# Statistics, decay chains, combining weights and the low-rank product of a fused encoder layer

## What is computed

```python
z = rms_norm(x, norm_mix_g) @ w_in           # all projections in one
gq, gk, gv, gg, gaf, gab, aq, ak, av, gate_a, gate_b = split(z)
# per direction; gaf, gab have 16 columns
la_f = log_sigmoid(gaf @ gla_wa2_f + gla_ba_f) / 16
la_b = log_sigmoid(gab @ gla_wa2_b + gla_ba_b) / 16
b  = cumsum(chunks(log_a))                   # gla_direction
qe, ke = q * exp(b), k * exp(-b)             # then chunked gated attention
o_a = rms_norm(o_f + o_b) * silu(gg)
# dilated attention, groups (window, dilation) = (128,1), (512,4), (2048,16)
o_g = softmax(q_g k_g^T / sqrt(128) - slope * dist) @ v_g     # with lse_g per query
wts = softmax(stack(lse_g), axis=0)          # over the three groups
o_att = sum(wts[g] * o_g)
merged = sigmoid(gate_a) * (o_a @ w_branch_a) + sigmoid(gate_b) * (o_att @ w_branch_b)
x += merged @ w_out;  x += relu(rms_norm(x) @ w1)^2 @ w2
x += sigmoid(rms_norm(x) @ w_pg) * (p @ w_pp)
```

## Time and profile before

| | us |
|---|---|
| three runs, median (lowest to highest) | 2895.54 (2891.09 to 2896.45) |
| the profiled execution | 2890.55 |
| its span, first to last instruction | 2889.0 |
| PE busy in the span | 2758.6 |
| DVE busy, ACT busy | 1172.1, 975.6 |

### The profile page before, as it was taken

How to read it: one execution, slowest core, us unless ns; L and a number is a source line. 1 busy time by engine, 2 the same in 40 slices (tenths; PEclk the granted TensorE clock), 3 DMA queues, 4 the chain that set the end, 5 groups by cost and what they waited for, 6 DMA issues and landing times.

```text
span 2889.0 us, 40495 instructions
## 1 busy us (share of the span) xinstructions
PE 2758.6 (95%) x14806; PEld 2365.4 (82%) x14806; DVE 1172.1 (41%) x1953; ACT 975.6 (34%) x1635; POOL 157.1 (5%) x248
## 2 busy tenths in 40 slices
PE   5999899998999899998999999999999999999798
PEld 5887788877888688886888888788888888888687
DVE  3234432344333433335433341645444544444533
ACT  4454135542454324443343332421121122122422
POOL 2000000010000100010010000000000000000000
PEclk9999999999999899999999999999999999999899
DMA  3122221231212212122162321111111111111021
GB/s 97 30 31 31 59 76 30 31 56 43 67 30 31 60 34 72 30 30 61 41 233 91 113 73 56 55 36 36 40 40 36 36 36 44 36 36 36 17 73 56
DMA packets 176575, 153.19 MB, mean 53 GB/s; under 512 B 13744, under 2 KB 155392, under 8 KB 176448
## 3 DMA queue, kind: packets, MB, share of 16 engines
q1 hardware_dynamic: 153824, 94.38, 12.0%
q0 software_dynamic: 16352, 57.00, 7.4%
q10 hardware_dynamic: 6272, 0.15, 0.1%
HBM read 127.48 MB, written 23.78 MB: 52 GB/s over the span
## 4 chain that ended last, share of the span: by engine, by line
PE 84%; DVE 6%; ACT 4%; issue 3%; DMA 2%; ACTq 0%; POOL 0%; DVEq 0%; SPq 0%; POOLq 0%
PE bank L695 24%; PE bank L697 24%; PE bank L696 24%; PE bank L802 2%; PE bank L783 1%; PE bank L884 1%; PE bank L871 1%; DMA work<-weight_scratch 1%; DVE work L1499 1%; PE bank L793 1%; PE bank L931 1%; DVE work L1479 1%; PE bank L845 1%; PE bank L880 1%; PE bank L770 1%
## 5 line engine op out<-in xcount | busy, mean ns | idle before, releaser
L695 PE MATMUL bank<-act_hi,w_hi 128*128 128x512 f32 (+1 forms) x3192 | 1189.4, 373 | 27.4 <-ACT work L1208 15.9
L697 PE MATMUL bank<-act_hi,w_lo 128*128 128x512 f32 (+1 forms) x3192 | 1140.9, 357 | 0.0
L696 PE MATMUL bank<-act_lo,w_hi 128*128 128x512 f32 (+1 forms) x3192 | 1140.9, 357 | 0.0
L695 PEld LDWEIGHTS bank<-act_hi,w_hi 128*128 128x128 f32 x3192 | 609.7, 191 | 112.5 <-ACT work L1208 17.3
L697 PEld LDWEIGHTS bank<-act_hi,w_lo 128*128 128x128 f32 x3192 | 608.2, 191 | 88.8
L696 PEld LDWEIGHTS bank<-act_lo,w_hi 128*128 128x128 f32 x3192 | 610.4, 191 | 75.7
L1016 ACT ACTIVATE w_hi<-w_raw 128x1024 fp32r<-128x1024 f32 (+2 forms) x179 | 180.1, 1006 | 435.3 <-PE bank L697 393.0
L1352 DVE TENSOR_TENSOR w_lo<-w_raw,w_hi 128x1024 fp32r<-128x1024 f32 (+2 forms) x181 | 210.9, 1165 | 232.2 <-ACT w_hi L1016 226.6
L695 PE MATMUL bank<-u_hi,w_hi 128*128 128x512 f32 (+1 forms) x816 | 289.6, 355 | 2.4 <-DVE work L1708 2.4
L696 PE MATMUL bank<-u_lo,w_hi 128*128 128x512 f32 (+1 forms) x816 | 289.5, 355 | 0.0
L697 PE MATMUL bank<-u_hi,w_lo 128*128 128x512 f32 (+1 forms) x816 | 289.0, 354 | 0.0
(11 more groups left out here) (224 smaller groups left out, 2399.9 us busy)
## 6 DMA issues: line engine op xcount, KB each, us to landing
w_raw<-in_w_in_dram SPq DMA_DIRECT2D x76, 512.0 KB, 3.9
w_raw<-in_w_mlp_dram SPq DMA_DIRECT2D x64, 512.0 KB, 3.8
gate_scratch<-work POOLq DMA_DIRECT2D x16, 640.0 KB, 3.2
work<-gate_scratch POOLq DMA_DIRECT2D x16, 640.0 KB, 6.5
work<-weight_scratch POOLq DMA_DIRECT2D x12, 640.0 KB, 6.5
oa_scratch<-work POOLq DMA_DIRECT2D x8, 640.0 KB, 5.1
work<-oa_scratch POOLq DMA_DIRECT2D x8, 640.0 KB, 8.3
x_in<-in_x_sample_dram SPq DMA_DIRECT2D x8, 512.0 KB, 8.0
```

Of the source, the lines that this page charges most:

```text
L695: nc.tensor.matmul(out, wh, rh, start=first and k == 0, stop=False, skip_group_check=True)
L696: nc.tensor.matmul(out, wh, rl, start=False, stop=False, skip_group_check=True)
L697: mm = nc.tensor.matmul(out, wl, rh, start=False, stop=k == kt - 1, skip_group_check=True)
```

## The change

Six things are done.

- The third group's statistics stay on the chip. Its transpose, copy and six stores are gone; the other two groups are stored to `stat_scratch` as [token, 4] and loaded back in the third group's query order by four DMAs; DVE uses `st` as it is. So the weights' rows also lie in query order, and the weighting reads them through a view that brings them to token order (`tokens`, `query_order`), in two instructions a group where there was one.
- `T_CW` goes from 292 to 264, and POOL stores and loads the weights before it refills the carry row. The rows for groups 0 and 1 lie in z rows 1 and 2, so ACT's evacuation of slab 13 waits for the combination (`ob_ready`).
- The combination stands at tick 303, between the two scans.
- The decay chains have a pair of rows each, and their steps interleave: both y, both Exp, then both Ln at tick 286, the scans at 292 and 317.
- The low-rank product is one fp32r matmul a chunk of 96 rows: high, low and high part of `lowrank` against low, high and high part of `wa2`. The parts of `wa2` are made once a head, at tick 100, by four ACT and two DVE instructions of 32 rows, those of `lowrank` once, ahead of the heads.
- v's transposes go to ticks 322 to 337, and the products with the chunk's end, both of them, to tick 341.

```diff
-        T_LR = (268, 287)
-        T_DECAY = (277, 334)
-        T_QK = (281, 339)
-        T_CW = 292
-        T_COMBINE = 318
-        T_VT = (332, 335, 338, 341, 344)
+        T_LR, T_Y, T_ABS, T_EXP, T_LN = (268, 275), (272, 280), (274, 282), (277, 285), 286
+        T_SCAN, T_DECAY, T_QK, T_KEND = (292, 317), (303, 328), (328, 335), 341
+        T_CW, T_COMBINE = 264, 303
+        T_VT, T_VN = (322, 325, 330, 334, 337), (327, 328, 334, 340, 341)
...
+        def query_order(row):
+
+            return (row.rearrange("p (j l n) -> p l n j", j=2, n=NT)[:, :, 0:8, :],
+                    row.rearrange("p (j l n) -> p l n j", j=8, n=NT)[:, :, 8:NT, :])
...
-        WB = (6, 7, 9)
+        wb_row = (work[:, 1, :], work[:, 2, :], ar[:, 9, :])
+        Y_ROW, B_ROW = (10, 2), (11, 7)
...
+                for j in range(2):
+                    pool.dma_start(cst[64 * j:64 * j + 64, 0:8, :], sample[j]).then_inc(cst_loaded, 16)
+                for b in range(2):
+                    pool.dma_start(cst[:, 8 + b, :], prompt[b]).then_inc(cst_loaded, 16)
...
                     for c, (t0, tw) in enumerate(CHUNKS):
-                        mm = nc.tensor.matmul(bank[(3, 4, 7)[c]][:, 0:tw], wa2[32 * d:32 * d + RANK, :],
-                                              lowrank[32 * d:32 * d + RANK, t0:t0 + tw], start=True, stop=True)
+                        mm = nc.tensor.matmul(bank[(3, 4, 7)[c]][:, 0:tw], wa2[:, d, :],
+                                              lowrank[:, t0:t0 + tw], start=True, stop=True)
...
+                if tick == T_LN:
+                    for d in range(2):
+                        A(ar[:, B_ROW[d], :], ar[:, B_ROW[d], :], ACT.Ln, bias=ones[:, 0:1]).then_inc(prep_a, 1)
...
+                        if tt == 13 and c == 0:
+                            act.wait_ge(ob_ready, h + 2)
...
                 if tick == T_CW:
-                    dve.wait_ge(cst_loaded, 16 * h + 16)
+                    dve.wait_ge(cst_loaded, 64 * h + 64)
+                    dve.wait_ge(exp_done, 30 * h + 31)
...
+                if tick == T_COMBINE:
+                    dve.wait_ge(wb_loaded, 48 * h + 48)
+                    for g in range(3):
+                        for o, w in zip(tokens(ar[:, 3 + g, :]), query_order(wb_row[g])):
+                            v_.tensor_tensor(o, o, w, ALU.mult).then_inc(dve_own, 1)
+                            dve.wait_ge(dve_own, own.value())
...
+                if tick in T_VN:
+                    i = T_VN.index(tick)
                     dve.wait_ge(gvt_done, 5 * h + i + 2)
...
+                if tick == T_KEND:
+                    dve.wait_ge(prep_a, 6 * h + 7)
+                    for d in range(2):
```

More of the change, by code:

```diff
@@ L26 @@
 P = 128
[L28 removed]
+MAP_BYTES = 212832
 EPS = 1e-6
@@ L575, in _ @@
                 nc.gpsimd.memset(carry[:, :, 0:1], 0.0).then_inc(carry_ready, 1)
[L576 removed]
+                for g in range(2):
                     store_stats(h, g)
[L579 removed]
+                pool.wait_ge(stat_stored, 16 * 8 * (h + 1) + 16)
                 pool.sem_inc(pool_passed, 1)
[L581 to L588, removed]
+                sample = stat_d[0:TS, :].rearrange("(l b j) m -> j l b m", b=8, j=2)
+                prompt = stat_d[TS:T, :].rearrange("(l b j) m -> b j l m", b=2, j=8)
+                for j in range(2):
+                    pool.dma_start(cst[64 * j:64 * j + 64, 0:8, :], sample[j]).then_inc(cst_loaded, 16)
+                for b in range(2):
+                    pool.dma_start(cst[:, 8 + b, :], prompt[b]).then_inc(cst_loaded, 16)
                 pool.wait_ge(cw_ready, h + 2)
@@ L1066, in _ @@
                 act.wait_ge(mm_done, c + 2)
-                A(lowrank[:, t0:t0 + tw], bank[c][0:48, 0:tw], ACT.Copy).then_inc(evac, 1)
+                for r0 in (0, 64):
+                    A(lowrank[r0:r0 + 32, t0:t0 + tw], bank[c][0:32, 0:tw], ACT.Copy).then_inc(lr_high, 1)
+            act.wait_ge(evac, 4)
             act.wait_ge(const_pool, 2)
@@ L1110, in gla_steps @@
             def gla_steps(h, tick):
+                if tick == T_WA2:
+                    act.wait_ge(head_loaded, 64 * (h + 1))
+                    act.wait_ge(lr_done, 2 * h + 1)
+                    for d, raw in enumerate((wa2_raw[32:64, :], wa2_raw[64:96, :])):
+                        A(wa2[32:64, d, :], raw, ACT.Copy)
+                        A(wa2[64:96, d, :], raw, ACT.Copy).then_inc(wa2_high, 1)
                 if tick == T_CW + 1:
@@ L1388, in _ @@
             x_lows(2)
+            for c, (t0, tw) in enumerate(CHUNKS):
+                dve.wait_ge(lr_high, 2 * c + 2)
+                v_.tensor_tensor(lowrank[32:64, t0:t0 + tw], bank[c][0:32, 0:tw], lowrank[0:32, t0:t0 + tw].bitcast(F32),
+                                 ALU.subtract).then_inc(evac, 1)
             dve.wait_ge(const_pool, 2)
@@ L1475, in gla_steps @@
                                      ALU.mult).then_inc(cw_ready, 1)
-                if tick == T_COMBINE:
-                    dve.wait_ge(wb_loaded, 48 * h + 48)
-                    for g in range(3):
-                        v_.tensor_tensor(ar[:, 3 + g, :], ar[:, 3 + g, :], ar[:, WB[g], :], ALU.mult).then_inc(dve_own, 1)
-                        dve.wait_ge(dve_own, own.value())
-                    v_.tensor_tensor(ar[:, 3, :], ar[:, 3, :], ar[:, 4, :], ALU.add).then_inc(dve_own, 1)
-                    dve.wait_ge(dve_own, own.value())
-                    v_.tensor_tensor(ar[:, WB[2], :], ar[:, 3, :], ar[:, 5, :], ALU.add).then_inc(ob_ready, 1)
```

163 lines of the change are left out of this document (89 added, 74 removed).

## The result

The changed kernel takes **2821.4 us** (median of 4 runs, 2820.9 to 2823.4), the kernel before in the same session 2896.0 (2891.1 to 2897.6): ratio 0.9744, 95% interval 0.9731 to 0.9758, 74.6 us less. The two profiled executions are 2890.55 and 2821.26 us, 69.3 apart. The forecast was 2836, its range 2812 to 2858.

A forecast was written before the change was run, and what follows sets the result against it. DVE's chain to v's first copy was taken to bound ticks 264 to 352: PE's floor 56.1, waits 0.2 and 7, half clock 2.8. From 81.0 to 66.2 us a head, times four 59 us, gives 2836 us, range 2812 to 2858.

The forecast's parts named there:

- Where: Ticks 264 to 352 of each head: 81.0 us become 66.2, 14.8 us a head; elsewhere nothing PE waits for changes.
- PE's floor: PE's own work at full clock in ticks 264 to 352: 59.7 us before, 56.1 after.
- The statistics and the transfer: Statistics loaded ahead of tick 264; the weights' 12.6 us store and load hidden, there 13 us before use: cost nothing.
- slower rival: DVE waits at tick 264 for late statistics loads, a loss from 15 us late on; 2920 us at worst, 6%.
- Scan 0: Its tick's work starts 23.8 us after tick 264, behind both Ln, an evacuation and `w_lo`; done at 29.9.
- The combination: DVE's weighting and additions after scan 0: 11.0 us with strided reads, bounds 8.1 and 13.7, ready at 40.9.
- The stall: PE at the third transposes (tick 330) waits for v's first copy from 42.0 to 49.0: 7 us, before about 10.8.
- The half clock: PE's slower clock after the stall at the third transposes: 2.8 us a head.
- ACT: Evacuation wait of 0.2 us at tick 320, before some 2.8 a head; ACT idle 5 us before slab 13, costing nothing.
- offset of 5 us: Added to the 2831.5 us forecast for the profiled execution, since the three runs' median before was 5 higher: 2836.
- the view costs little: Strided weighting nearly free: combination 8.1 us, stall 4, window 61.6 to 63.4, 2818 to 2825 us; 13%.
- DVE isn't the bound: v's first copy ready at 42, 7 us sooner; window 56.1, gain 24.9 a head, 2796 us; 5%.

The follow-up runs named there:

- serial_chains: Changed kernel with the two directions' decay chains one after the other, scan 0 at tick 282, four table loads a head: 2793.2 us.
- late_weights: Changed kernel with the making of the weights (`T_CW`) moved from tick 264 back to 290: 2874.6 us.
- plain_view: Changed kernel with the weighting as one contiguous instruction a group, weights not in token order: 2812.8 us.
- fp32_lowrank: Changed kernel with the low-rank product as plain fp32 over 16 rows again: 2839.6 us.
- both_undone: Changed kernel with `T_CW` back at 290 and the low-rank product as plain fp32 of 16 rows again: 2896.4 us.

## Why the prediction was right

By its own steps, per head:

- **Where.** It said that all of the gain lies in ticks 264 to 352, and that there the path to v's first copy decides. The windows give 69.8 us where the profiled executions differ by 69.3, and each experiment moved the time through that stall or through PE's own work.
- **PE's floor**, 56.1. Measured 56.8 with no wait and full clock (serial_chains): 0.7 low. The product's 0.6 is 0.58.
- **The statistics and the transfer.** Costed at nothing: DVE waits 0.30 us for no DMA at 578.80, and the weights are there some 14 us ahead of the combination (the last load is issued at 587.3 and the longest landing takes 6.9 us: 594.2 against 608.28), where 13 was said. No new wait at ticks 96 to 110 is among PE's waits. The slower rival had no part.
- **Scan 0** was to start at t = 23.8, behind both Ln, an evacuation and the rounding. Measured 24.0. This step was right in its reason too, and it was the most expensive row of the changed kernel: I took it as given and did not ask what it costs. Serial_chains, which starts this step 9.8 us sooner, is 6.7 us a head faster.
- **The combination**, 11.0 us, bounds 8.1 and 13.7. Measured 9.1: 1.33 us for a 1024-wide weighting where 1.9 was said, near the 1.2 that I had named as a sign of being wrong, and 0.65 for a 256-wide one where 0.6 was said. This is the term that was mis-sized. I took the 0.68 ns an element of a strided write in rows 7 for all 1280 columns; it is 0.10 for the 1024 (two interleaved streams, each advancing by one word) and 0.86 for the 256 (eight of them). The row that I took for the whole holds, roughly, for a fifth of it.
- **The stall.** PE came at 42.3 where 42.0 was said; the copy was ready at 46.9 instead of 48.9; 4.65 us instead of 7, by the 1.9 of the combination and a few tenths. So the stall gave back 6.1 us a head where 3.8 was said.
- **The half clock**, 2.8 us. What is left above floor and stall is 63.55 - 56.8 - 4.65 = 2.1. It is an error of its own, since the runs don't show that it goes with the length of the stall (2.0 us behind stalls of 17.8 in late_weights, 1.6 behind 3.1 in plain_view); the 2.8 was taken from one stall of before.
- **ACT.** PE waits for no evacuation at ticks 312 and 320 (0.2 was said). ACT is idle 3.60 us before slab 13, where 5 was said, and PE doesn't notice.

The sum: 56.1 + 0.2 + 7.0 + 2.8 = 66.1 was predicted (66.2 by the walk), 56.8 + 0 + 4.65 + 2.1 = 63.55 came. Four times 2.65 is 10.6 of the 14.6 us between 2836 and 2821.4. There was some luck in it: the floor was 0.7 too low where all else was too high, by 3.25 together. Most of the rest is the offset of 5 us (4.5 as rounded) that I carried over from the median of before to the profiled run of before; the changed kernel's median and its profiled run agree within 0.2 us. That offset was scatter of the kernel before, and no property of the sum.

Of the rivals, "the view costs little" had the right mechanism, with 8.1 us for the combination and 2818 to 2825 for the kernel; the combination lies between it and the forecast, the time in it. "DVE isn't the bound" needed the copy 7 us sooner; it came 2.0 sooner. The same rival is what serial_chains reached, in another way: its 2796 stands against 2793.2.

On the Trainium skill's rule, "Vector Engine (DVE) Microarchitecture Reference", section 5.2, which the prediction weighed: one source that hops at every element costs 1.73 ns a column by it. Its hops are of 4 KiB, those of the view of 2.5 KiB (two streams, 640 words apart) and 640 bytes (eight). The 256-wide part agrees roughly, 0.86 ns more an element where the rule has 0.68. The 1024-wide part doesn't, 0.10. Neither part comes to the 2.50 that the prediction also weighed. The same section notes that a one-source operation with a read stream that alternates between two regions ran at full rate, and calls the penalty not simply one for each hop; I had passed over that sentence, and it is the one that comes nearest to the two interleaved streams here. That the number of streams decides, and not the distance between them or the length of a run, no run here shows.

What each part is worth, from the runs: the early weights 53 us and the one matmul 18, each undone alone; together 75.0 (2896.4 - 2821.4), where the 3.6 us above their sum are mostly half clock behind low-rank groups, as far as the one trace of each shows. The view costs 8 to 9 us in the changed kernel, and the interleaving, with scan 0's place behind the weight split, 28. All the rest of the change together, with late weights and the slow product, costs 6 us against the kernel before. That is a loss and a gain: with late weights too the serial chains are 24.3 us faster than the interleaved ones (2850.3 against 2874.6), so something else in the rest gains about what the interleaving and the view cost. Which part it is (a pair of rows for each direction, the combination ahead of scan 1, the earlier transposes), no run shows. The third group's statistics were not undone alone. The row of line 581 above says what they are for: going through memory as before, they would have held the weights back to more than 23 us behind tick 264. How much of the 53 us would be left then stays open.

## What to carry to other kernels

Read an engine's queue for the work that stands in front of the first step of the long chain, and not only for the waits that a change removes: here direction 0's Ln waited for direction 1's Exp, to save two table loads of 1.28 us a head, and scan 0 for a weight split behind it; together they kept 28 us from the kernel. A small transfer through memory (12 us here) belongs at the first tick at which its data exist: here it cost nothing there and its full length in the middle of the chain. It can pay to change where the data come from, so that this tick comes sooner. And a saving on an engine is worth what the waiting engine still waits: 1.5 us a head of DVE's time were 8.6 us in one kernel and none in the next.

## What the runs showed of the hardware

- **Strided reads of one source.** With two interleaved streams, 1329 against 1225 ns for 1024 columns; with eight, 646 against 425 ns for 256. The prediction had one price for both.
- **Half clock behind a stall.** In head 1 of the changed kernel a stall of 4.62 us was followed by some 3 us at 1.2 GHz, in the heads 3, 0 and 2 by some 4.0, 4.4 and 5.3 us (by the lengths of the 256-wide matmuls, 0.41 us against 0.28), after stalls of the same length. In plain_view three heads with 3.1 us of stall show 0.97 and the fourth 1.00.
- **Half clock behind a 16-row fp32 group.** In fp32_lowrank one such group of eight was followed by it, in both_undone groups of three heads out of four, with the same instructions in front. What decides it I have not found. Behind one group it costs some 1.5 us, and 3.1 us in the head where both groups are followed by it (t = 46.2, 47.7 and 49.3 at the third transposes).
- **Matmul shapes.** Six plain fp32 passes of 16 rows take 2.34 us from start to start, three fp32r matmuls of 96 rows 0.58 for the same columns, four times less.
